# Logits of the next pair issued ahead of this pair's tails and transposes in a two-block attention kernel

## What is computed

```python
def hybrid_layer(x, w_in, w_out, ln_g, ln_b, rel_bias, topk):
    proj = jnp.einsum('bsd,dn->bsn', x, w_in)
    qA, kA, vA, gA, qB, kB, vB, gB, qI, kI, wI = jnp.split(proj, SPLIT_POINTS, axis=-1)
    oA = stick_breaking_attention(heads(qA, HEADS_A), heads(kA, HEADS_A), heads(vA, HEADS_A))
    oB = dsa_sparse_attention(heads(qB, HEADS_B), heads(kB, HEADS_B), heads(vB, HEADS_B), ...)
    mix = jnp.concatenate([oA * jax.nn.silu(gA), oB * jax.nn.silu(gB)], axis=-1)
    return layer_norm(ALPHA * x + jnp.einsum('bsm,md->bsd', mix, w_out), ln_g, ln_b)

# stick-breaking, strictly causal
z = jnp.einsum('bqhd,bshd->bhqs', qb, k) * scale
log_rest = jnp.where(strict, jax.nn.log_sigmoid(-z), 0.0)
tail = lax.cumsum(log_rest, axis=3, reverse=True) - log_rest
a = jnp.where(strict, jnp.exp(jax.nn.log_sigmoid(z) + tail), 0.0)
```

## Time and profile before

| what | value |
|---|---|
| three timed runs | 2978.09, 2983.62, 2988.78 us; median 2983.62 us |
| profiled execution | 2977.82 us in all, span 2976.1 us |
| busy in the span | TensorE 2409.9 us, VectorE 1745.8 us, POOL 982.1 us, ScalarE 911.2 us |
| stage 0, stage 1, stage 2 | from 1602, 2168 and 2660 us to the end at 2976 us |
| granted TensorE clock over the execution | 0.89 |

### The profile page before, as it was taken

One profiled execution on the slowest core, in us unless ns is written; L12 is line 12 of the kernel. 1 busy time (PEld: TensorE's weight loads), 2 busy tenths in 40 slices (PEclk: granted clock), 3 DMA queues, 4 the chain that ended last, 5 costly groups with the idle time before them and its releaser, 6 DMA issues. The chain is left out here.

```text
span 2976.1 us, 30377 instructions
## 1 busy us (share of the span) xinstructions
PE 2409.9 (81%) x9779; PEld 1614.1 (54%) x9779; DVE 1745.8 (59%) x3656; ACT 911.2 (31%) x1742; POOL 982.1 (33%) x691
## 2 busy tenths in 40 slices
PE   6997999869878888898786996798557467549897
PEld 4776878758663334343333654575345345437574
DVE  3444311032136988988875678587759869865151
ACT  4444222233322222222212433143234314323232
POOL 2332555343232244344342234224323532420001
PEclk9998999989989999999898997899768778769898
DMA  4321333223139899999999899899799999965553
GB/s 158 98 67 50 96 98 102 79 83 124 52 125 343 313 407 413 415 412 397 395 414 404 325 370 356 343 365 393 303 358 373 416 406 377 386 268 196 216 190 140
DMA packets 257323, 805.56 MB, mean 271 GB/s; under 512 B 18366, under 2 KB 139862, under 8 KB 191655
## 3 DMA queue, kind: packets, MB, share of 16 engines
q0 software_dynamic: 73728, 536.90, 44.8%
q1 hardware_dynamic: 183463, 267.06, 25.6%
...
## 5 line engine op out<-in xcount | busy, mean ns | idle before, releaser
L1337 POOL DMA_INDIRECT gathered<-in_peer_rows,experts x436 | 530.4, 1216 | 923.5 <-DVE x_res L2630 616.3
L1695 PE MATMUL peer_banks<-gathered,peer_diags 128*128 128x512 f32 x720 | 338.3, 625 | 53.1 <-ACT peer_diags L1750 53.1
L78 PE MATMUL group_banks<-group_x_t,group_ring 128*128 128x128 f32 (+1 forms) x2016 | 342.9, 334 | 15.9 <-ACT group_x_t L2442 8.4
L78 PEld LDWEIGHTS group_banks<-group_x_t,group_ring 128*128 128x128 f32 x2016 | 310.1, 210 | 46.7 <-ACT group_x_t L2442 10.8
L2616 DVE CUSTOM_DVE_ANT_0 gathered<-gathered,late_nat 128x1024 f32<-128x1024 f32 x256 | 315.6, 1235 | 33.2 <-DMA gathered<-in_peer_rows,experts 28.1
L2630 DVE SCALAR_TENSOR_TENSOR x_res<-gathered,group_weights,x_res 128x1024 f32<-128x1024 f32 x256 | 328.3, 1283 | 2.7 <-DVE group_weights L2622 0.3
L1695 PEld LDWEIGHTS peer_banks<-gathered,peer_diags 128*128 128x128 f32 x720 | 142.5, 201 | 238.3 <-issue 238.3
L2256 PE MATMUL group_banks<-group_ring,group_x_t 128*128 128x512 f32 x512 | 235.7, 616 | 23.2 <-DMA group_ring<-in_weights 23.2
L1790 DVE CUSTOM_DVE_ANT_0 peer_product<-gathered,early_nat 128x1024 f32<-128x1024 f32 x180 | 214.7, 1223 | 37.8 <-DMA gathered<-in_peer_rows,experts 37.7
L1695 PE MATMUL peer_banks<-early_gathered,peer_diags 128*128 128x512 f32 x304 | 150.4, 647 | 53.4 <-ACT peer_diags L1750 53.4
L2256 PEld LDWEIGHTS group_banks<-group_ring,group_x_t 128*128 128x128 f32 x512 | 99.1, 198 | 146.5 <-issue 118.9
...
## 6 DMA issues: line engine op xcount, KB each, us to landing
...
```

The costliest lines, as they stand in the source:

```text
L78: last = nc.tensor.matmul(out, lhsT, rhs, start=n == 0, stop=n == len(pairs) - 1)
L1337: nc.gpsimd.indirect_dma_start(row_buffer(m, r), None, A["peer_rows"], bass.IndirectOffsetOnAxis(ap=at, axis=0))\
L1695: last = nc.tensor.matmul(ps[:, ACC[unit % 2] + half, :], diags[:, r % DIAGS, :], row_buffer(m, r)[:, D + half * BANK:D + (half + 1) * BAN ...
```

## The change

TensorE issues the next unit's logits directly after that unit's projection, ahead of this unit's `tails` or `turn_weights`. `stick_out(u)` and `sparse_out(u)` come one unit later, the last one after the loop. In the last stick unit, `natural("v")` stands behind `sparse_logits` and `tails`. The buffers of the soft logits become two: `near_part(u)` gives `work[:, 0]` for even and `work[:, 2]` for odd units, and `suffix` gets a second part. ScalarE's list follows: `softplus(u+1)` before `stick_weights(u)`, with the gelus of a point between them, and `copy_pair(u+1)` before `sparse_weights(u)`. For unit 1, `softplus` waits until the index scores, which use the same part of `work`, are summed.

```diff
@@ -1988,6 +1988,10 @@
     def pair_banks(u):
         return 2 + 2 * (u % 2)
 
+    def near_part(u):
+
+        return 2 * (u % 2)
+
     with ctx:
         ps = banks()
         ring = sb("ring", [P, WS, D])
@@ -1999,7 +2003,7 @@
         values = [sb(f"values{half}", [P, last + 1, HALF]) for half in range(2)]
         work = sb("work", [P, 3, 2, SC])
         share = sb("share", [P, NT, HALF])
-        suffix = sb("suffix", [P, 2, 2 * P]) if NT == 1 else None
+        suffix = sb("suffix", [P, 2, 2, 2 * P]) if NT == 1 else None
         bias = sb("bias", [P, 2, 2, SC])
         score, keep = sb("score", [P, max(len(searched), 1), ROW_W[last]]), sb("keep", [P, SC])
         best = sb("best", [P, NT, 8])
@@ -2295,7 +2299,7 @@
                 def tails(l, u):
                     pe.wait_ge(soft_ready, PAIRS * l + u + 1)
                     for e in range(2):
-                        bank, soft = ps[:, pair_banks(u) + e, :], work[:, 0, e, :]
+                        bank, soft = ps[:, pair_banks(u) + e, :], work[:, near_part(u), e, :]
 
                         def later(at, source):
                             return nc.tensor.matmul(bank[:, at:at + source.shape[-1]], m.neg_ones[:, :].bitcast(F32), source,
@@ -2305,7 +2309,7 @@
                         if NT == 2:
                             made = later(P, soft[:, 2 * P:3 * P])
                         else:
-                            later(0, suffix[:, e, 0:(last - 1) * P])
+                            later(0, suffix[:, u % 2, e, 0:(last - 1) * P])
                             made = later((last - 1) * P, soft[:, last * P:(last + 1) * P])
                     made.then_inc(tail_done, 1)
 
@@ -2397,24 +2401,27 @@
                     natural(l, "g", STICK)
                     for u in range(PAIRS):
                         pair(l, u + 1)
-                        tails(l, u)
                         if u + 1 < PAIRS:
                             stick_logits(l, u + 1)
                         else:
+                            sparse_logits(l, PAIRS)
+                        tails(l, u)
+                        if u + 1 == PAIRS:
                             natural(l, "v", SPARSE)
-                            sparse_logits(l, PAIRS)
-                        stick_out(l, u)
+                        if u:
+                            stick_out(l, u - 1)
+                    stick_out(l, PAIRS - 1)
                     for u in range(PAIRS, UNITS):
                         if u + 1 < UNITS:
                             pair(l, u + 1)
+                            sparse_logits(l, u + 1)
                         turn_weights(l, u)
-                        if u + 1 < UNITS:
-                            sparse_logits(l, u + 1)
                         if u == PAIRS:
                             natural(l, "g", SPARSE)
-                        sparse_out(l, u)
-                        if u == PAIRS:
                             turn_mix(l, STICK)
+                        else:
+                            sparse_out(l, u - 1)
+                    sparse_out(l, UNITS - 1)
                     turn_mix(l, SPARSE)
                     output(l)
 
@@ -2486,7 +2493,7 @@
 
                 def softplus(l, u):
                     n = PAIRS * l + u
-                    z, near = ps[:, pair_banks(u):pair_banks(u) + 2, 0:SC], work[:, 0, :, :]
+                    z, near = ps[:, pair_banks(u):pair_banks(u) + 2, 0:SC], work[:, near_part(u), :, :]
                     act.wait_ge(logits_done, UNITS * l + u + 1)
                     nc.scalar.activation(near, z, ACT.Abs).then_inc(soft_step, 1)
                     act.wait_ge(soft_step, 3 * n + 1)
@@ -2571,11 +2578,13 @@
                     for u in range(PAIRS):
                         copy_pair(l, u + 1)
                         done = gelus((l, "stick", u, 0), done)
+                        if u + 1 < PAIRS:
+                            if u == 0 and searched:
+                                act.wait_ge(summed, SCORES * (l + 1))
+                            softplus(l, u + 1)
+                        done = gelus((l, "stick", u, 1), done)
                         stick_weights(l, u)
-                        done = gelus((l, "stick", u, 1), done)
-                        if u + 1 < PAIRS:
-                            softplus(l, u + 1)
-                        else:
+                        if u + 1 == PAIRS:
                             done = copy_values(l, SPARSE, done)
                         done = gelus((l, "stick", u, 2), done)
                         done = gelus((l, "stick", u, 3), done)
@@ -2583,17 +2592,17 @@
                     for u in range(PAIRS, UNITS):
                         p = u - PAIRS
                         if p == 0:
+                            copy_pair(l, u + 1)
                             sparse_weights(l, u)
-                            copy_pair(l, u + 1)
                             copy_turned(l, u)
                             done = gates(l, SPARSE, done)
                             done = gelus((l, "gate1"), done)
                             copy_mix(l, STICK)
                         else:
-                            sparse_weights(l, u)
-                            done = gelus((l, "sparse", p, 0), done) if p else done
                             if u + 1 < UNITS:
                                 copy_pair(l, u + 1)
+                            sparse_weights(l, u)
+                            done = gelus((l, "sparse", p, 0), done)
                             copy_turned(l, u)
                         done = gelus((l, "sparse", p, 1), done)
                         done = gelus((l, "sparse", p, 2), done)
@@ -2687,7 +2696,7 @@
 
                 def soft(l, u):
                     n = PAIRS * l + u
-                    near = work[:, 0, :, :]
+                    near = work[:, near_part(u), :, :]
                     dve.wait_ge(soft_step, 3 * n + 3)
                     made = nc.vector.scalar_tensor_tensor(out=near, in0=ps[:, pair_banks(u):pair_banks(u) + 2, 0:SC], scalar=0.0, in1=near,
                                                           op0=ALU.max, op1=ALU.add)
@@ -2695,7 +2704,7 @@
                         dve.drain()
                         later = near[:, :, last * P:(last + 1) * P]
                         for i in range(last - 1, 0, -1):
-                            into = suffix[:, :, (i - 1) * P:i * P]
+                            into = suffix[:, u % 2, :, (i - 1) * P:i * P]
                             made = nc.vector.tensor_tensor(into, near[:, :, i * P:(i + 1) * P], later, ALU.add)
                             later = into
                             if i > 1:
```

## The result

The changed kernel takes 3012.52 us (median of 4 runs, 3005.73 to 3021.30) against 2986.20 us for the kernel before in the same comparison (4 runs, 2978.09 to 2988.78): a ratio of 1.0093, with an interval of 1.0069 to 1.0117. I had predicted 2983.3 us and a range up to 2996. It is slower, beyond my range.

A forecast was written before the change was run, and what follows sets the result against it. Stages 0 and 1 (token tiles 0-1 and 2) were taken as paced by VectorE's row products and their transfers, stage 2 (tile 3) by TensorE. +5.0 - 2 - 3.8 + 0.5 = -0.3 us gave 2983.3 us, range 2968 to 2996.

The forecast's parts named there:

- Copy of the pair in stage 2: Logits directly behind the projection wait for its copy: 0.70 us a pair, seven pairs, +4.9 us a layer.
- New waits at `pair(6)` and before the transposes: Stage 2: 0.9 us for the gates' bank, about 0.4 us at transposes of units 4, 5 and 6; together +2.1 us.
- Walking one layer of stage 2 through: Check of stage 2 by stepping through one layer: the same as the summed terms, +5.0 us for two layers.
- Last outputs: Stages 0 and 1, out(6) between turn(7) and out(7): +1.9 us at most, 0 at least, taken as +0.5 us.
- Nothing is charged for the waits before tails and transposes: Stages 0 and 1: VectorE's rows hide these waits before and after; without that cover the 28 copies would cost 20 us.
- softplus gain: Stage 0: logits before soft(1) start earlier without the tails ahead, 0.95 us a layer, -2 us.
- smaller waits behind the gates: Stages 0 and 1: sparse gate projection starts about 1.55 us earlier, shortening VectorE's gelu waits; -3.8 us over four layers.
- the logits two pairs on need it: Stages 0 and 1: the tails' exponential, now behind a gelu, is needed only by logits issued a whole pair later.
- The signs: Wrong if stages 0 and 1 move over 10 us, stage 2's clock falls below 0.92, or stage 2 gets shorter.
- Rival 3: ScalarE's queue becomes the wait, copy_pair(u+1) standing ahead of sparse_weights(u) and gelus: slower, 3006 us, half of it 2997; chance 0.12.
- Rival 2: TensorE keeps full clock through a shorter wait before stage 0's gate projection: 2980 us; chance 0.10.
- Rival 1: Stages 0 and 1: gelu wait behind the gates goes in all four layers, at most -40 us, 2949 us; chance 0.16.

The follow-up runs named there:

- e5: Changed kernel with the late output behind the next pair's logits, ahead of the unit's tails or transposes: 2998.4 us, 1.0039 of before.
- e4: Changed kernel with the late output between the next pair's projection and its logits: 2989.2 us, 1.0006 of before.
- e11: The change's order in stages 0 and 1 alone, stage 2 in the order of the kernel before: 2996.3 us, 1.0017 of before.
- e2: Changed kernel with out(6) on TensorE ahead of turn(7) instead of behind it: 3006.1 us, 1.0076 of before.
- e8: As e4, with the sparse gate projection ahead of turn(4) on TensorE in stages 0 and 1: 2985.7 us, 0.9996 of before.
- e10: As e8, with the sparse gates and their gelus also ahead of copy_turned(4) on ScalarE in stages 0 and 1: 2988.6 us, 0.9997 of before.

## Why the prediction was wrong, step by step

*Copy of the pair in stage 2, +4.9 us a layer.* Right: seven new waits of 0.54 us a layer stand in the changed profile, and e5 against e4 measures 4.6 and 2.7 us.

*New waits at `pair(6)` and before the transposes, +2.1.* The first 0.80 us against 0.9, the second 0.27 us each where I had 0.4. Right, but among what goes I had wrongly counted the 1.11 us before `out(7)`: 1.17 us are there with the change. With what goes, these made +2.5 us a layer; e5, the change without the outputs' wait, measures +3.3 and +2.3 us a layer against before.

*"Walking one layer of stage 2 through ... gives the same."* This is the step that failed. My walk let `stick_weights` start when its tails were done and `copy_turned` when its transposes were, and never asked for the third condition in the code, that the output of the unit before has read the buffer. Before, that condition was always met first, so no row of the trace showed it. It cost 7.1 and 7.8 us in stage 2's layers, part of it through TensorE's clock, which I had taken as unchanged there: about 3.2 of the 5 us at the first layer's end.

*"Last outputs": `out(6)` between `turn(7)` and `out(7)`, "+1.9 us at most, 0 at least", taken as +0.5.* Wrong by the same omission: I priced the moved matmuls, not the copy that must follow them. In stage 2 this stretch grew by 5.0 us a layer. I had not even put it into stage 2's part.

*Stages 0 and 1: "Nothing is charged for the waits before tails and transposes"; -0.3 us with stage 2.* Wrong by sign. The softplus gain (3.1 us against 2; e11, with the same order in stage 0, has 1.4) and the smaller waits behind the gates (4.1 us against 2.3 in stage 0) are both in the trace. But the prediction names nothing of what passes the value projection: `logits(4)`, with a key copy behind a gelu, went ahead of 13.9 us of projection, on which the next gelu hangs. The two waits are one budget. By layer, behind the values and behind the gates together: before 18.0 us in stage 0 (0 + 9.91, 0 + 8.08), in the change 25.1 (6.68 + 6.76, 4.54 + 7.10), and in e4, with the projection as late but W gone, 18.3 (4.14 + 5.83, 0 + 8.32). So the later value projection only handed the wait from one place to the other, and the change's other 7 us are gone where the output lies between projection and logits. The 4.7 us more at the start of the second layer are TensorE's clock, 0.69 against 0.90, and came back in e2 with `out(6)` ahead of `turn(7)`: a price of the last outputs again, in a place where I had not looked for it. The 1.5 us at the start of the first layer come and go between executions whatever the order.

*The sentence "the logits two pairs on need it, and these are issued a whole pair of VectorE's work later"* was true and beside the point: the logits were not the reader that mattered.

*The signs.* I had said that I was wrong if the clock in stage 2 fell below its 0.92; it fell to 0.90.

*The rivals.* Rival 3, ScalarE's queue, had the right engine, sign and nearly the size (2997 to 3006 us at a chance of 0.12), and the wrong instruction: it looked at `copy_pair` ahead of `sparse_weights`, whose price is the 0.27 us above. Rival 2 was half right in stage 0: after a wait of 0.82 us instead of 5.16 the gate projection ran at full clock, 13.90 us where it had been 15.5, but stage 0 got no shorter; as I read the trace, because VectorE was late by then for another reason. Rival 1 did not come: even e8 and e10, which moved the gate projection itself, gained nothing that can be told. Its price was too high from the start: it took 9.91 us for all four layers, and in stage 1 only 3.5 and 4.2 us stand behind the gates. The Trainium skill's rule ("Trainium Kernel Development and Optimization", Key Constraints) that issued transfers share the 16 DMA engines would have taken 2.3 of the 3.8 us for the gates out of my sum. Stage 1 of e8 and e10 agrees with that outcome, with gelu waits gone and row waits up by 6.6 and 6.5 us, though no run here separates the engines' share from the order of the transfers in the queue.
